# A two-layer hybrid trunk with a mixture of experts: layer 1 with 4 large and 12 small experts, down weights issued one position later, each tile's rows gathered, added and normed by itself

## The chip, the cores and the metric
The kernel runs on one core of one Trainium2 chip. The time is the device time of one execution in microseconds (us); the median of three runs is given. One more execution was recorded by the profiler, and all rows come from that one.

## The reference
Two layers are applied to 256 context tokens and 256 latent tokens of width 1024, all in float32. A layer has a mixing half (retention, Mamba-2 and neighbourhood attention behind one input projection, then an output projection) and a mixture of experts. The change is in the second half of each layer, and in the norm ahead of either half:

```
def moe_ffn(h, router_w, router_b, w_gate, w_up, w_down):
    ...
    for e in range(N_EXPERTS):
        he = jax.nn.silu(t @ w_gate[e]) * (t @ w_up[e])
        out = out + gates[:, e:e + 1] * (he @ w_down[e])
```

There are 16 experts with a hidden width of 512, and each token has two of them, so `gates` has two values that aren't zero in a row. `h` becomes `h + g_f * moe_ffn(modulate(rmsnorm(h)))`. Layer 0 does this for all 512 tokens, layer 1 for the 256 latent ones alone.

## The kernel before, in words
Tokens lie in tiles of 128 (`NT` = 4 tiles; `tiles(l)` gives 4 tiles in layer 0 and tiles 2 and 3 in layer 1). Semaphores order everything by hand; each engine has its own program.

*Routing.* `route` and `assign` (DVE) choose two experts for each token, count the tokens of each, and rank the experts by load; experts 0 and 1 are put at ranks 0 and 1 always, since their weights are loaded before the router has run. The first `BIG` = 8 ranks are large, with room for 128 tokens, the other 8 small, with room for 64 (`SMALL_CAP`). `rounds` (L1800) says how many rounds are needed until all tokens have had a place; `order_i` (L1806) lists the expert of each position, in one copy.

*Positions.* A round goes through 16 positions q. `RANKS` mixes them: two large, two small, and so on. Two small experts that stand side by side share one gather of 128 token rows; such a group, or one large expert, is a unit (`UNITS`, `NU` = 12). For each unit DVE finds the token of each slot (`slots_of`, `who`), POOL gathers the rows (`gather`, L2053), PE turns them (`turn_x`, L1037) and ACT copies them (L1343).

*PE in a round.* For each q, in this order: gate weights of q (`wide(r, q, 0)`), turning of the product of q-1 (`turn_h`, L1069), up weights of q (`wide(r, q, 1)`), at a unit's first position the turning of the next unit's rows, and down weights of q-1 (`down`). A large expert has 16 matmuls of 512 columns in each of gate (L1060), up (L1060) and down (L1087); a small one has its two halves side by side, gate and up at L1057 with 32 matmuls of 256 columns, down at L1082 with 16 of 512. ACT does silu and the copy of the turned product, DVE the product of gate and up (L1858) and the copy of the result (L1866); ACT then stores the rows of the result (L1365 in two pieces for a small expert, L1368).

*SP and the weights.* There are six slots of 2 MB: gate, up and down for even positions and the same for odd ones. The weights of position q+2 go where those of q were. The four loads that experts 0 and 1 can have early, and the last two of expert 0, are issued ahead of the round. Then a loop over pairs of positions reads the expert's number from `order_i` and, for gate, up and down in turn, waits until PE has finished that product of q-2 (`gate_pe`, `up_pe`, `dn_pe`) and issues the load (`load_expert`, L590). SP's instructions run in order, so a load also waits for the waits of all loads ahead of it.

*The end of a round.* When all rows are stored, POOL gathers for each tile its second choice, then for each tile its first (`sum_order`; two gathers per tile, four buffers, L2074). DVE adds each, times the token's gate, to `tokA`, which ACT has set to zero before the round (L1335, L1911). After the last round DVE multiplies each tile by the gate row (L1940), and the addition to `h` is done by POOL for even tiles (L2079) and DVE for odd ones (L1944).

*Norms.* `square_rows` (ACT, L1158) sums the squares of each tile; `norm_rows` (DVE) waits for all tiles, scales them (L1450), waits for POOL's power (`rsqrt`, L1978), and scales the tiles (L1454); PE then turns them (L683).

## Time and profile before

| | us |
|---|---|
| median of 3 runs | 1457.79 |
| the three runs | 1447.16, 1457.79, 1470.85 |
| the profiled execution | 1446.61 |
| its span, first to last instruction | 1444.8 |
| PE busy in the span | 1239.8 (86%) |
| weight loads of PE (beside its matmuls) | 673.2 |
| DVE, ACT, POOL busy | 409.9, 223.1, 139.9 |
| mean granted clock of PE | 0.931 of full |
| read from and written to HBM | 309.84 MB, 16.79 MB |

The experts of layer 0 run from about 469 to 777, their end with the next norm to 818, the experts of layer 1 from about 1112 to 1421 and their end to 1444.8. A busy PE is a PE with matmuls in flight. The granted clock is 1.00 at 2.4 GHz and 0.5 at 1.2 GHz; a stretch between them has both.

### The profile page before, as it was taken

The page shows a single profiled execution, that of the slowest core. Times are in us where ns is not written, and L with a number is a line of the kernel's source. Part 1 is how long each engine was busy: PE and PEld are TensorE (multiplying, and loading weights), DVE is VectorE, ACT ScalarE, POOL GpSimd, SP SyncE. Part 2 cuts the span into 40 slices and gives each one's busy share as a digit, 9 for nine tenths or more (in the row PEclk, how much of TensorE's full clock was granted, in tenths as well). Part 3 has the DMA queues.
Part 4 walks back from the last instruction along what each step waited for, and adds up shares of the span by engine and source line. Part 5 has one row for each costly group of instructions (what it writes and reads, how often), then busy time and mean ns, then how long its engine had stood idle before and what let it go on. Part 6 is the DMA issues. An engine that isn't in the chain of part 4 may idle for free.

```text
span 1444.8 us, 14245 instructions
## 1 busy us (share of the span) xinstructions
PE 1239.8 (86%) x5712; PEld 673.2 (47%) x5712; DVE 409.9 (28%) x737; ACT 223.1 (15%) x412; POOL 139.9 (10%) x119
## 2 busy tenths in 40 slices
PE   4999999999994798989894399989993999989892
PEld 1444446676543354545442256547642444535351
DVE  0130125863225312121102621247325110111103
ACT  2121121112204110101000212221213100101010
POOL 0002112620000100000002202114000000000001
PEclk8899998799997899999997699999996999999997
DMA  9311125434604469899988222245374389999984
GB/s 365 134 58 59 59 109 218 169 117 175 291 5 171 160 261 391 363 385 367 400 339 298 71 65 110 103 191 202 117 291 170 135 347 363 374 383 370 384 351 147
DMA packets 34238, 327.53 MB, mean 227 GB/s; under 512 B 5632, under 2 KB 5632, under 8 KB 16512
## 3 DMA queue, kind: packets, MB, share of 16 engines
q1 hardware_dynamic: 23328, 292.03, 50.8%
q0 software_dynamic: 5184, 18.88, 3.9%
q10 hardware_dynamic: 5664, 15.73, 2.8%
q8 instruction: 46, 0.75, 0.2%
q14 instruction: 16, 0.13, 0.0%
HBM read 309.84 MB, written 16.79 MB: 226 GB/s over the span
## 4 chain that ended last, share of the span: by engine, by line
PE 76%; DMA 11%; DVE 6%; ACT 3%; issue 2%; POOL 1%; SPq 1%; ACTq 0%; DVEq 0%; POOLq 0%
PE ps L1060 16%; PE ps L720 13%; PE ps L1087 7%; DMA ring<-in_w_gate 6%; PE ps L964 6%; PE ps L707 6%; PE ps L1057 4%; PE ps L653 3%; PE ps L1082 2%; PE ps L877 2%; DMA ring<-in_w_mod 2%; PE ps L1037 2%; PE ps L893 1%; PE ps L921 1%; PE ps L638 1%
## 5 line engine op out<-in xcount | busy, mean ns | idle before, releaser
L720 PE MATMUL ps<-ring,featT 128*128 128x512 f32 (+1 forms) x480 | 186.9, 550 | 0.0
L1060 PE MATMUL ps<-ring,arena 128*128 128x512 f32 x256 | 127.6, 658 | 27.9 <-DMA ring<-in_w_gate 25.5
L720 PEld LDWEIGHTS ps<-ring,featT 128*128 128x128 f32 x480 | 90.7, 190 | 92.3 <-issue 89.9
L1060 PE MATMUL ps<-arena 128*128 128x512 f32 x256 | 113.3, 595 | 2.4 <-ACT arena L1343 2.4
L1087 PE MATMUL ps<-arena 128*128 128x512 f32 x256 | 113.7, 597 | 0.0
L1858 DVE TENSOR_TENSOR arena<-arena,ps 128x512 f32<-128x512 f32 (+1 forms) x32 | 17.7, 555 | 338.1 <-PE ps L1060 237.2
L1060 PEld LDWEIGHTS ps<-ring,arena 128*128 128x128 f32 x256 | 53.1, 213 | 97.5 <-issue 66.7
L707 PE MATMUL ps<-featT,ring 128*128 128x512 f32 (+1 forms) x192 | 82.6, 589 | 2.3 <-ACT featT L1168 2.3
L964 PE MATMUL ps<-ring,featT 128*128 128x512 f32 x192 | 82.7, 592 | 0.0
L1866 DVE COPY arena<-ps 128x1024 f32<-128x1024 f32 (+1 forms) x32 | 30.6, 958 | 164.5 <-PE ps L1087 109.0
L2053 POOL DMA_INDIRECT arena<-ffn_rows,slot_i x24 | 23.7, 989 | 538.8 <-DVE slot_i L1850 538.8
L1060 PEld LDWEIGHTS ps<-arena 128*128 128x128 f32 x256 | 47.4, 190 | 60.9 <-issue 60.9
L1350 ACT ACTIVATE arena<-ps 128x512 f32<-128x512 f32 (+1 forms) x32 | 15.7, 490 | 377.5 <-PE ps L1060 214.9
L1087 PEld LDWEIGHTS ps<-arena 128*128 128x128 f32 x256 | 47.4, 190 | 54.3 <-issue 54.3
L1057 PE MATMUL ps<-arena 128*64 128x256 f32 x512 | 58.8, 382 | 7.5 <-DMA arena<-in_w_up 7.3
L683 PE MATMUL ps<-const,tokA 128*128 128x128 f32 x112 | 20.1, 358 | 49.2 <-DVE tokA L1454 47.5
L1082 PE MATMUL ps<-arena 128*64 128x512 f32 x256 | 58.3, 595 | 4.3 <-ACT arena L1357 4.3
L1057 PE MATMUL ps<-ring,arena 128*64 128x256 f32 x512 | 58.8, 382 | 0.0
L707 PEld LDWEIGHTS ps<-featT,ring 128*128 128x128 f32 x192 | 36.8, 194 | 46.0 <-issue 42.7
L964 PEld LDWEIGHTS ps<-ring,featT 128*128 128x128 f32 x192 | 36.5, 190 | 45.9 <-issue 45.9
L1057 PEld LDWEIGHTS ps<-arena 128*64 128x64 f32 x512 | 38.9, 137 | 28.0 <-issue 15.2
L653 PE MATMUL ps<-ring,silT 128*32 128x256 f32 (+1 forms) x656 | 50.7, 431 | 0.0
(276 smaller groups left out, 1403.0 us busy)
## 6 DMA issues: line engine op xcount, KB each, us to landing
arena<-in_w_down SPq DMA_DIRECT2D x32, 2048.0 KB, 11.1
ring<-in_w_mod SPq DMA_DIRECT2D x21, 2048.0 KB, 7.7
arena<-in_w_gate SPq DMA_DIRECT2D x16, 2048.0 KB, 13.9
arena<-in_w_up SPq DMA_DIRECT2D x16, 2048.0 KB
ring<-in_w_gate SPq DMA_DIRECT2D x16, 2048.0 KB, 14.3
ring<-in_w_up SPq DMA_DIRECT2D x16, 2048.0 KB, 18.8
ring<-in_w_in SPq DMA_DIRECT2D x10, 2048.0 KB, 8.0
ring<-in_w_out SPq DMA_DIRECT2D x4, 2048.0 KB, 8.1
```

Source lines behind the costliest of these rows:

```text
L653: i = mm(mod_row(l, u)[g:g + 32, :], silT[:, k, :], piece(q)[:, k, c:c + mod_width(l)], start=k < 4, stop=k >= 4)
L707: o = mm(bank[:, lo:TOK], W[:, k, c:c + P], featT[:, k, lo:TOK], start=k == 0, stop=k == KD - 1)
L720: o = mm(bank[:, lo:hi], featT[:, k, P * i:P * i + P], W[:, k, lo:hi], start=k == 0, stop=k == KD - 1)
L877: i = mm(ps[:, 6 + t // 2, 256 * (t % 2):256 * (t % 2) + 256], featT[:, k, P * t:P * t + P], nvw[:, k, :], start=k == 0, stop=k == KD - 1)
L964: i = mm(ps[:, 4 + n % 2, :], featT[:, k, P * t:P * t + P], piece(p)[:, k, :], start=k == 0, stop=k == KD - 1)
L1037: o = tr(ps[:, 5 + k // 4, P * (k % 4):P * (k % 4) + P], gathered[u % 2][:, P * k:P * k + P], ident)
L1057: o = mm(ps[64 * half:64 * half + 64, m, 0:256], X_[:, k, at:at + SMALL_CAP], W[:, k, 256 * half:256 * half + 256], start=k == 0, stop=k = ...
L1060: o = mm(ps[:, m, :], X_[:, k, :], W[:, k, :], start=k == 0, stop=k == KD - 1)
L1082: o = mm(ps[64 * out_half:64 * out_half + 64, 3, :], hT[:, b, 64 * half:64 * half + 64], W[:, k, 512 * out_half:512 * out_half + 512], sta ...
L1087: o = mm(ps[:, 3 + out_half, :], hT[:, k, :], W[:, k, 512 * out_half:512 * out_half + 512], start=k == 0, stop=k == 3)
L1866: V.tensor_copy(Yb[:, q % 2, 0:n], flat(3, n)).then_inc(S("y_dve"), 1)
L2053: G.indirect_dma_start(gathered[u % 2], None, rows_in[l], bass.IndirectOffsetOnAxis(slot_i[:, u % 2:u % 2 + 1], 0)).then_inc(S(f"gathered{ ...
```

## The change
There are three parts. (1) A `Plan` for each layer takes the place of `BIG`, `RANKS` and `UNITS`: layer 0 keeps its order, layer 1 has 4 large and 12 small experts, in 10 units. `Round` holds what the semaphores have counted before a round, as the layers now count differently. (2) SP issues the down weights of a position behind the gate and up weights of the next. (3) The rows come back tile by tile: ACT scales the row of the second choice into `tokA` (no zeroing any more), DVE adds the first choice, multiplies by the gate row and adds to `h`, within the round, for all tiles; POOL adds nothing. The norms split the tiles into all but the last and the last.

```diff
-BIG = 8
+BIGS = (8, 4)
...
-        UNITS = [u for j in range(NE // 4) for u in ((4 * j,), (4 * j + 1,), (4 * j + 2, 4 * j + 3))]
-        RANKS = [v for j in range(NE // 4) for v in (2 * j, 2 * j + 1, BIG + 2 * j, BIG + 2 * j + 1)]
-        NU = len(UNITS)
...
+            def units(self):
+
+                out, q = [], 0
+                while q < NE:
+                    n = 2 if self.small(q) else 1
+                    out.append(tuple(range(q, q + n)))
+                    q += n
+                return out
...
+            def runs(self):
+
+                starts = [q for q in range(NE) if q == 0 or self.ranks[q] != self.ranks[q - 1] + 1]
+                return [(a, b, self.ranks[a]) for a, b in zip(starts, starts[1:] + [NE])]
+
+        PLANS = (Plan(BIGS[0], [v for j in range(4) for v in (2 * j, 2 * j + 1, 8 + 2 * j, 9 + 2 * j)]),
+                 Plan(BIGS[1], [0, 1, 4, 5, 6, 7, 2, 3, 8, 9, 10, 11, 12, 13, 14, 15]))
...
-                with sp.Fori(1, R * (NE // 2)) as i:
-                    for c in range(2):
-                        e = sp.value_load(order_i[0:1, bass.ds((i % (NE // 2)) * 2 + c, 1)], min_val=0, max_val=NE - 1)
-                        for j, name in enumerate(("gate_pe", "up_pe", "dn_pe")):
-                            sp.wait_ge(S(name), first * NE + i * 2 + (c - 1))
-                            load_expert(e, c, j)
...
+                def wide_weights(behind, e, c):
+
+                    for j, name in enumerate(("gate_pe", "up_pe")):
+                        sp.wait_ge(S(name), first * NE + behind)
+                        load_expert(e, c, j)
+
+                def down_weights(behind, e, c):
+
+                    sp.wait_ge(S("dn_pe"), first * NE + behind)
+                    load_expert(e, c, 2)
+
+                wide_weights(1, expert_at(2), 0)
+                with sp.Fori(0, more * (NE // 2) + (NE // 2 - 2)) as i:
+                    e = [expert_at(i * 2 + 2 + n) for n in range(3)]
+                    wide_weights(i * 2 + 2, e[1], 1)
+                    down_weights(i * 2 + 1, e[0], 0)
+                    wide_weights(i * 2 + 3, e[2], 0)
+                    down_weights(i * 2 + 2, e[1], 1)
...
-                A(tokA[:, t0:NT, :].rearrange("p t (k c) -> p (t k) c", c=P), repeat(ONE, T * KD), ACT.Identity, scale=0.0
-                  ).then_inc(S("acc_zero"), 1)
...
+                    for i in range(T):
+                        t = t0 + i
+                        act.wait_ge(S(f"back{2 * i % 4}"), backs(l, 2 * i, first, n_round))
+                        A(tokA[:, t, :], back[2 * i % 4], ACT.Identity, scale=gate2[:, 1, t:t + 1]).then_inc(S("half_act"), 1)
...
-                V.tensor_copy(rounds[:, l:l + 1], few[:, 1:2]).then_inc(S("rounds_dve"), 1)
+                link(V.tensor_copy(rounds[:, l:l + 1], few[:, 1:2]))
+                V.tensor_scalar(rounds[:, DEPTH + l:DEPTH + l + 1], few[:, 1:2], -1.0, None, ALU.add).then_inc(S("rounds_dve"), 1)
...
-                V.tensor_copy(order_i.rearrange("p (j h c) -> p h j c", h=2, c=2),
-                              load_of.rearrange("p (h j c) -> p h j c", h=2, c=2)).then_inc(S("order_dve"), 1)
+                for a, b, v in plan.runs():
+                    i = V.tensor_copy(order_i[:, a:b], load_of[:, v:v + b - a])
+                i.then_inc(S("order_dve"), 1)
...
+                    for i in range(T):
+                        t, q = t0 + i, 2 * i + 1
                         dve.wait_ge(S(f"back{q % 4}"), backs(l, q, first, n_round))
+                        dve.wait_ge(S("half_act"), ended(l, first, n_round, i + 1))
+                        V.scalar_tensor_tensor(tokA[:, t, :], back[q % 4], gate2[:, 0, t:t + 1], tokA[:, t, :], ALU.mult, ALU.add
+                                               ).then_inc(S("both_dve"), 1)
+                        dve.wait_ge(S("both_dve"), ended(l, first, n_round, i + 1))
+                        V.tensor_tensor(tokA[:, t, :], tokA[:, t, :], grow[:, t // 2, :], ALU.mult).then_inc(S("gated_dve"), 1)
+                        dve.wait_ge(S("gated_dve"), ended(l, first, n_round, i + 1))
+                        V.tensor_tensor(h[:, t, :], h[:, t, :], tokA[:, t, :], ALU.add).then_inc(S("h_end"), 1)
...
-                    for q, (n, t) in enumerate(sum_order(l)):
-                        if q >= 4:
-                            pool.wait_ge(S("acc_dve"), added(l, first, n_round, q - 3))
+                    for q in range(2 * T):
+                        i, n = q // 2, 1 - q % 2
+                        if i >= 2:
+                            used = "half_act" if n else "both_dve"
+                            pool.wait_ge(S(used), ended(l, first, n_round, i - 1))
                             step_on()
...
-                for n in range(0, T, 2):
-                    pool.wait_ge(S("ffn_dve"), upto("ffn_dve", l, n + 1))
-                    G.tensor_tensor(h[:, t0 + n, :], h[:, t0 + n, :], tokA[:, t0 + n, :], ALU.add
-                                    ).then_inc(S("h_end0"), 1)
```

## Rows read from the trace of the kernel before
**Rows 1.** Waits of PE (engine, line, releaser: us, times, longest), 1120 to 1421, layer 1
```profile
PE ps L1060 <- DMA ring<-in_w_gate: 12.2, 3, 4.3
PE ps L1057 <- DMA arena<-in_w_up: 3.8, 3, 1.4
```
**Rows 2.** Waits of PE, 478 to 778, layer 0's experts
```profile
PE ps L1060 <- DMA ring<-in_w_gate: 13.4, 3, 5.4
PE ps L1057 <- DMA arena<-in_w_up: 3.5, 3, 1.4
```
**Rows 3.** PE in order of time (start, us, what), layer 1, positions 4 to 8
```profile
1194.14 9.93 PE L1060 MATMUL ps<-ring,arena 128*128 128x512 f32 x16 [3.92 <-DMA ring<-in_w_gate]
...
1215.67 7.13 PE L1060 MATMUL ps<-arena 128*128 128x512 f32 x16
...
1238.01 3.67 PE L1057 MATMUL ps<-ring,arena 128*64 128x256 f32 x32
...
1253.92 3.67 PE L1057 MATMUL ps<-arena 128*64 128x256 f32 x32
...
1259.12 3.67 PE L1057 MATMUL ps<-arena 128*64 128x256 f32 x32 [1.16 <-DMA arena<-in_w_up]
1262.60 3.63 PE L1082 MATMUL ps<-arena 128*64 128x512 f32 x16
1270.18 8.83 PE L1060 MATMUL ps<-ring,arena 128*128 128x512 f32 x16 [3.95 <-DMA ring<-in_w_gate]
...
1416.63 3.65 PE L1082 MATMUL ps<-arena 128*64 128x512 f32 x16 [2.12 <-ACT arena L1357]
```
**Rows 4.** SP's DMA issues in order of time, layer 1, positions 2 to 4
```profile
1161.85 0.33 SPq L590 DMA_DIRECT2D arena<-in_w_down  x1
...
1177.76 0.33 SPq L590 DMA_DIRECT2D arena<-in_w_down  x1
1179.46 0.34 SPq L590 DMA_DIRECT2D ring<-in_w_gate  x1
```
**Rows 5.** Windows of layer 1: us, busy by engine, then PEclk, DMA share, GB/s
```profile
1180.00:1213.00 33.00, 27.66 (x113) 13.63 (x111) 3.13 (x7) 2.54 (x5) 0.00 (x0) 0.90 0.99 415
1190.00:1202.00 12.00, 8.08 (x14) 3.48 (x13) 1.87 (x4) 0.00 (x0) 0.00 (x0) 0.72 1.00 426
1202.00:1212.00 10.00, 10.00 (x33) 4.92 (x31) 0.69 (x1) 0.87 (x2) 0.00 (x0) 1.00 1.01 434
```
**Rows 6.** DMA issues of layer 1's experts: count, KB each, us to landing
```profile
arena<-in_w_down SPq DMA_DIRECT2D x14, 2048.0 KB, 11.1
...
expert_rows<-arena ACTq DMA_DIRECT2D x8, 512.0 KB, 11.0
expert_rows<-arena ACTq DMA_DIRECT2D x14, 128.0 KB, 9.3
```
**Rows 7.** All engines in order of time, end of layer 0's experts
```profile
788.70 2.54 DVE L1911 SCALAR_TENSOR_TENSOR tokA<-arena,tokA 128x1024 f32<-128x1024 f32 x2 [0.81 <-DMA arena<-expert_rows,arena]
...
798.47 2.53 DVE L1911 SCALAR_TENSOR_TENSOR tokA<-arena,tokA 128x1024 f32<-128x1024 f32 x2 [0.75 <-DMA arena<-expert_rows,arena]
...
801.47 2.36 DVE L1940 TENSOR_TENSOR tokA<-tokA,arena 128x1024 f32<-128x1024 f32 x2 [0.22 <-DVE arena L1936]
...
809.42 3.25 DVE L1944 TENSOR_TENSOR h<-h,tokA 128x1024 f32<-128x1024 f32 x1
...
815.21 2.74 DVE L1454 TENSOR_SCALAR tokA<-h,stat 128x1024 f32<-128x1024 f32 x4 [1.16 <-POOL stat L1978]
...
818.00 5.12 PE L683 MATMUL ps<-const,tokA 128*128 128x128 f32 x32 [40.77 <-DVE tokA L1454]
```
**Rows 8.** All engines in order of time, end of layer 1's experts
```profile
1432.88 2.48 DVE L1911 SCALAR_TENSOR_TENSOR tokA<-arena,tokA 128x1024 f32<-128x1024 f32 x2 [0.57 <-DMA arena<-expert_rows,arena]
...
1438.19 3.25 DVE L1944 TENSOR_TENSOR h<-h,tokA 128x1024 f32<-128x1024 f32 x1
```
**Rows 9.** DVE, the router's chain of layer 0
```profile
463.21 0.17 DVE L1806 CAST order_i<-arena 128x16 int32<-128x16 f32 x1
```

More of the change, by code:

```diff
@@ L496, in opens, with ended, summed @@
-        def opens(q):
-            return q in [qs[0] for qs in UNITS]
-        def small(q):
-            return RANKS[q] >= BIG
-        def first_row(q):
-            v = RANKS[q]
-            return P * min(v, BIG) + SMALL_CAP * max(v - BIG, 0)
-        def stores(q):
-            return 16 * sum(2 if small(p) else 1 for p in range(q % 2, q + 1, 2))
-        STORES = stores(NE - 1)
+        def ended(l, first, n_round, n):
+            return first * NT + n_round * len(tiles(l)) + n
+        def summed(l, first, R, left=0):
+            return first * NT + R * len(tiles(l)) + (NT - left)
@@ L567, in _ @@
                     if l > 0 and m == 2:
-                        for w in ("h_end0", "h_end1"):
-                            sp.wait_ge(S(w), upto(w, l - 1, len(tiles(l - 1)) // 2))
+                        sp.wait_ge(S("h_end"), summed(l - 1, first, R))
                         layer_rows(l)
@@ L2089, in _ @@
                 if l > 0:
-                    for w in ("h_end0", "h_end1"):
-                        pool.wait_ge(S(w), upto(w, l - 1, len(tiles(l - 1)) // 2))
+                    pool.wait_ge(S("h_end"), summed(l - 1, first, R))
+                    pool.sem_inc(S("pool_steps"), 1)
                 for c in (0, CTX + 1):
```

269 lines of the change are left out of this document (150 added, 119 removed).

## The prediction
> **What bounds the kernel now.** I read four views in this order: who waited for whom on PE in the two expert stages, PE and SP in order of time over four expert positions, the windows with their DMA rate, and the two ends where the experts' rows are collected. The expert stages are the part that the change touches most, and they hold two fifths of the span. In layer 1 (1122 to 1421) PE waits 12.2 us for gate weights and 3.8 us for up weights, and in layer 0 13.4 and 3.5 us [rows 1, 2]. Nearly all else in the stage is PE work. The reader is to see the price of one period of four positions in [rows 3]: position 4 starts at 1194.14, position 8 at 1270.18. The stages of PE (gate of q, turning, up of q, down of q-1) cost, from start to start: a large expert behind a large one 22.3 us (1215.67 to 1238.01); a small one that opens a unit, behind a large one, 15.9 (1238.01 to 1253.92); a small one behind a small one 12.3 less a wait of 1.2, so 11.1; a large one behind a small one 21.5, less 2.8 that its gate took too long, so 18.7. Sum 68.0 us of PE work in a period of 76.0 (75.3 in the others). The gate that follows the wait of 3.9 us runs at 1.2 GHz for a while: 9.93 and 8.83 us where 7.1 is usual [rows 3], with the granted clock at 0.72 in that stretch and 1.00 in the next [rows 5]. So PE bounds the stage, with about 7 us of DMA wait and its clock loss in each period.
>
> Why do weights come late when transfers idle elsewhere? SP issues gate, up and down of position q+2 in that order, and each waits for its slot. At 1161.85, as PE ends down 0 and begins gate 2, SP issues the down weights of position 2; at 1177.76 those of position 3; and only 1.7 us later the gate of position 4 [rows 4]. PE had left that gate's slot when gate 2 was done, 3.67 us (a small gate [rows 3]) after 1161.85, at 1165.5. The gate load stood 14 us behind a down load that waited for PE's down 1.
>
> **Down weights one position later, both layers.** The new SP order (gate q+1, up q+1, down q) is the order in which PE leaves the slots, so nothing stands behind a wait that is not its own. It issues the same 42 loads; only the order and the addresses' register loads change, three of these at a loop's head, while SP waits for PE anyway (uncovered they would cost 1 us or so each time: the gap from down to the next gate is 1.7 us with one of them [rows 4]). No new wait stands on PE, ACT or DVE.
>
> Layer 0: what can go is 16.9 us of waits [rows 2] and three times 1.7 us of slow gate (8.83-7.13, from the gates in [rows 3]), 22.0 us. What is late next is the transfer rate. A period moves 12 loads of 2.097 MB, three gathers and two stores of 0.524 MB, and two stores of 0.262 MB (two pieces of 128 KB) [rows 6]: 28.3 MB. Busy stretches move 415 GB/s mixed and 434 with weights alone [rows 5], so 28.3/0.415 = 68.2 us against 68.0 of PE. That is a tie, but gate and up of positions 3 and 4 now leave some 10 to 15 us ahead, and a deficit of 0.2 us a period doesn't use this up. I take 21 us. Bounds: at 400 GB/s (4% under the 415, my low end for a queue that is never idle) a period needs 70.8 us and the gain is 22-8 = 14; it can't exceed 22.
>
> **Four large experts in layer 1.** Experts 0 and 1 always hold two of the four large places, so one round is enough only while the third largest of the other fourteen has at most 64 tokens. By the reference, the third largest load of all sixteen in layer 1 is 60, 44 and 43 for seeds 0, 1 and 2, so one round stays. Work removed on PE: positions 2 to 15 are now s s s s L L and eight s. With the stages above (an opening s behind s is 12.2: 11.1 and the turning of x): 15.9+11.1+12.2+11.1+18.7+22.3+15.9+11.1+12.2+11.1+12.2+11.1+11.1+11.1 = 187 us, where it was 231. From the end of down 0 at 1161.8 PE alone would end at 1349, and with the last turning and down (6 us) at 1355, against 1416.63+3.65 = 1420.3 now [rows 3, 4].
>
> But a small position releases its slots each 11 to 12 us and refills them with 6.29 MB, half a gather and a small store, 6.8 MB, 16.4 us at 415 GB/s. So transfers take over as the bound. In the times of before: the down load of position 2 is issued at 1161.85 as now; gate 4 and up 4 follow at 1165 and 1170; down 3 at 1177.76 starts at about 1178.7, and from there the queue always has a next load (in the two large stages PE takes 41.0 us where transfers need 2x17.7; the lead of 15 us from positions 3 to 5 covers the 5.6). Left then are 35 loads, 73.4 MB; five gathers, 2.6; stores of three large (1.6) and ten small positions (2.6): 80.2 MB. At 415 GB/s 193.3 us, so the last weights are in at 1372.0, PE sees them about 1 us later and needs 3.65 us for the last down: 1376.7. Gain 43.6; I take 43. Bounds: at 400 GB/s 200.5 us, gain 36; at 434 184.8 us, gain 52.
>
> A rule on this. Rows show 415 to 434 GB/s for HBM to SBUF with the engines' share at 0.99 to 1.01 [rows 5]. The Trainium skill (DMA: Bandwidth & Descriptors, Where 436 GB/s comes from) says that between HBM and SBUF the HBM side binds at some 358 GB/s and only the fabric reaches 435. By that rule 80.2 MB take 224 us and layer 1 gains 13 us instead of 43; the trace disagrees on this core with its 415, so it only makes one of the rivals.
>
> **Router's chain.** The order is copied in eight pieces in layer 0 and four in layer 1, in place of one of 0.17 us [rows 9], and the rounds get one more small instruction. At 0.1 us each, between nothing (they don't wait for one another) and 0.17: with the small one 0.9 and 0.5, on the path, since the first one-hot waits behind them; bounds 0.3 and 2.2 together. I take 1.5. The dropped zeroing on ACT ran beside this chain: nothing.
>
> **Rows gathered, added and normed by tile, end of layer 0.** Before, DVE takes the eight rows as they land, at 1.28 us each, and the last ends at 801.0; only then come the multiplications by the gate row (1.18 each) and the additions, at 3.25 each while POOL adds beside, up to 809.42+3.25 = 812.67; PE starts at 818.00 [rows 7]. After: ACT scales the first row of a tile, DVE does 1.28+1.18+an addition. Nothing shows an addition of this shape with POOL quiet: it lies between 1.18 (the multiplication, same shape) and 3.25; I take 1.2, as POOL no longer adds. Tile 0 can start at 788.70, when its second row is in; four tiles of 3.75 with their hand-overs end at 803.7. The last gathers wait for buffers as before and are in at about 800, hidden. Then square, power and one scaling (0.69 of the 2.74 for four [rows 7]) in place of four: 5.3 us become about 4.7, since three scalings still queue ahead on DVE. PE starts at 808.5 to 809. Gain 9, bounds 1 (additions of 3.25) and 11.
> The same split before each expert stage saves three and one scalings, less the queue: 1.1 and 0.7 us; bounds 0 and 3 together.
>
> **End of layer 1.** The last row is consumed at 1435.4, h is ready at 1441.4 [rows 8]. After: tile 0 (second row in at about 1431) ends at 1434.8, tile 1 at 1438.5. Gain 2.9, bounds -0.5 and 4.
>
> **Sum.** 43+21+9+1.8+2.9-1.5 = 76 us. The profiled execution took 1446.6, so 1370.4 for one like it. The three timed runs had a median of 1457.8, 11 us above it, and the lowest 1447.2 is at it. I put the new median at 1377, some half of that excess kept.
>
> **Rivals.** (A) As summed, 1377. (B) Transfers do worse when they are never idle (400 GB/s; a refill bubble of a microsecond in each position would do the same): 36+14+12 = 62 us, 1391. For it: a stretch with PE, gathers and stores at once moves 415, not 434. Against: the rate didn't fall within those stretches. (C) They do better, 434 as with weights alone: 52+22+13 = 87 us, 1366. Against: stores and gathers are always there. (D) HBM can't sustain the rate of a short stretch, and a period's mean of now, 28.3 MB in 75.3 us or 376 GB/s, is the ceiling: layer 1 needs 213 us for its 80.2 MB and gains 23, layer 0 nothing, the ends 12: 1457.8-35 = 1423. Against: 33 us on end at 415 [rows 5]. The page above gives such a ceiling; with its 358 the estimate would be 1433, within the bound of no change. (E) The clock, and this one ends on the other side. In layer 1 PE waits for every load, about 1.5 us three times a position. If this kept it at 1.2 GHz, small stages would take 22 us, above the 16.4 of the transfers: the twelve small stages, 187-41 = 146 us, become 292, and the stage ends near 1161.8+292+41+12 = 1507, 86 us later than before. With the other gains (33) that is 53 us over the median of before: 1511. Against no change it decides where the stage ends at 1420.3+33 = 1453, with 1453-1161.8-41-12 = 238 us for the 146: a granted clock near 0.6 over the small positions. For it: waits of 3.9 us brought 0.72 [rows 3, 5]. Against: the wait of 1.2 before an up and of 2.1 before the last down left 3.67 and 3.65 us, full speed [rows 3], and a PE that runs slower waits less. The Trainium skill (TensorE: Matmul & The Clock Gate, HAM oscillation — how this bites in real kernels) describes just such a loop, less work per load than wait, where each tile starts cold; by it E is what happens, by the short waits in the trace it isn't. (F) The change needs a second round in layer 1 after all: another 250 us, over 1620; it decides at 65 tokens for that third expert.
>
> **Chances.** A 0.57, B 0.20, C 0.15, D 0.04, E 0.03, F 0.01. A, B and C are faster by over 2% (29 us, about what a measurement of this kernel can tell from no change): 0.92 with them. So is most of D, to 1423; its lower ceilings are within 2%, and with the near side of E that makes 0.04. Slower, from E and F: 0.04. Range 1357 to 1402: from C with a run as fast as the profiled one, to B with all of the median's excess.
>
> **What would show it.** Right: in layer 0 no wait of PE for gate weights, and periods of 68 to 69 us; in layer 1 waits of 1 to 2 us before most products from about position 9 on, a DMA share of 0.98 or more with 410 to 420 GB/s from 15 us behind down 0 to the last load, a granted clock above 0.95, and a stage that is 43 us shorter; each tile's addition near 1.2 us, and PE in the next projection's turning some 9 us sooner behind the last down of layer 0. Wrong: waits for gathers or stores in place of those for weights, a rate of 400 GB/s or less, small gates of 7 us, additions of 3.25, or SP late at its loop's head.

## The result, and the profile after

The changed kernel takes 1375.07 us (median of 4 runs, 1366.9 to 1378.24), the kernel before 1454.97 in the runs beside it: a ratio of 0.9459, with a 95% interval of 0.9392 to 0.9526. Every ratio below is to the kernel before in the runs beside it. The forecast was 1377.0. The profiled execution took 1374.44 us, its span is 1372.6, 72.2 less than before, and its mean granted clock is 0.931 as before.

The span splits at events that both kernels have. "G1" is the gate product of a layer's second expert, which opens the steady part of the experts; "owner" is the first small matmul that finds a slot's token. The router's chain stands ahead of it, so its price is forecast in the rows that end at an owner.

| stretch of the span, us | before | after | gain | forecast |
|---|---|---|---|---|
| start to layer 0's first owner | 468.8 | 468.5 | 0.3 | 0.2 |
| owner to G1, layer 0 | 28.1 | 28.2 | -0.1 | 0 |
| G1 to the last down product, layer 0 | 280.4 | 258.1 | 22.3 | 21 |
| from there to PE's turning for the next norm | 40.8 | 31.0 | 9.8 | 9 |
| middle: from there to layer 1's first owner | 294.6 | 299.7 | -5.1 | 0.2 |
| owner to G1, layer 1 | 26.8 | 28.3 | -1.5 | 0 |
| G1 to the last down product, layer 1 | 280.8 | 237.1 | 43.7 | 43 |
| end of layer 1 | 24.5 | 21.6 | 2.9 | 2.9 |

The four large terms came within 1.3 us each; what was not forecast is the row of the middle stage, whose instructions are the same but for the split norm and the router's copies in its last part. Small rows are to be read with care: in ten profiles with the same code up to layer 0's first owner (the changed kernel and the experiments below that leave this stretch alone) it took 464.2 to 471.5 us, and one kernel had 470.8 and 464.2.

**Layer 0.** Waits of PE, 455 to 756 us (line, releaser: us in all, times, longest), which answer to [rows 2]:

```profile
PE ps L1091 <- DVE arena L1918: 13.9, 2, 11.3
PE ps L1076 <- DVE arena L1839: 5.9, 1, 5.9
PE ps L1100 <- DMA arena<-ffn_rows,slot_i: 2.6, 1, 2.6
PE ps L1123 <- ACT arena L1407: 2.4, 2, 1.2
PE ps L1145 <- ACT arena L1421: 2.1, 1, 2.1
```

No wait for a weight load is left: the 13.4 and 3.5 us of [rows 2] are gone. The first two lines are the router's chain, ahead of the experts. PE in order of time, at the start of two periods:

```profile
545.94 3.27 PE L1123 MATMUL ps<-ring,arena 128*128 128x512 f32 x7
...
613.92 2.41 PE L1123 MATMUL ps<-ring,arena 128*128 128x512 f32 x5
```

That is 68.0 us for four positions, where 76.0 stood in [rows 3] for layer 1 of before, and the window over it shows what carries it:

```profile
546.00:614.10 68.10, 68.10 (x301) 33.67 (x300) 13.53 (x20) 6.75 (x11) 2.81 (x3) 1.00 1.00 415
```

PE is busy for all 68.10 us at a granted clock of 1.00 while the DMA engines are at a share of 1.00 with 415 GB/s. It is the tie that the forecast described, with both sides busy throughout; these rows don't show which would end first.

**Layer 1.** Waits of PE, 1085 to 1347 us, which answer to [rows 1]:

```profile
PE ps L1145 <- DMA arena<-in_w_down: 6.6, 4, 2.6
PE ps L1120 <- DMA arena<-in_w_up: 3.8, 3, 2.2
PE ps L1100 <- DMA arena<-ffn_rows,slot_i: 3.3, 1, 3.3
PE ps L1120 <- DMA arena<-in_w_gate: 2.5, 2, 1.3
PE ps L1123 <- ACT arena L1407: 2.4, 2, 1.2
PE ps L1120 <- DMA ring<-in_w_gate: 2.3, 2, 1.2
PE ps L1120 <- DMA ring<-in_w_up: 2.3, 2, 1.1
```

PE in order of time, from position 11 on, and the end:

```profile
1267.61 3.67 PE L1120 MATMUL ps<-arena 128*64 128x256 f32 x32 [1.27 <-DMA arena<-in_w_gate]
...
1273.84 5.36 PE L1120 MATMUL ps<-arena 128*64 128x256 f32 x32 [2.18 <-DMA arena<-in_w_up]
...
1284.09 3.67 PE L1120 MATMUL ps<-ring,arena 128*64 128x256 f32 x32 [1.16 <-DMA ring<-in_w_gate]
...
1326.24 5.26 PE L1145 MATMUL ps<-arena 128*64 128x512 f32 x16 [2.64 <-DMA arena<-in_w_down]
...
1341.19 3.65 PE L1145 MATMUL ps<-arena 128*64 128x512 f32 x16 [1.68 <-DMA arena<-in_w_down]
...
1347.34 3.65 PE L1145 MATMUL ps<-arena 128*64 128x512 f32 x16 [2.12 <-ACT arena L1421]
```

The lead lasts until position 11, two later than forecast. From there PE waits 1.1 to 1.7 us before most products and still runs them at full speed (3.67 us), as [rows 3] had it; only behind the two longest waits, 2.18 and 2.64 us, does a product take longer (5.36 and 5.26 us). The first of these starts at full speed: the granted clock is 0.96 in its first 1.16 us and 0.52 in the 3.45 us after that. The windows of this stage:

```profile
1153.00:1345.00 192.00, 174.45 (x1060) 93.49 (x1056) 22.55 (x47) 16.52 (x32) 4.68 (x5) 0.98 1.00 424
1160.00:1340.00 180.00, 163.64 (x982) 87.75 (x978) 21.91 (x45) 15.78 (x30) 4.68 (x5) 0.98 1.01 427
```

The transfers hold 427 GB/s for 180 us, above the 415 of the sum.

**End of layer 0.** DVE, then PE, in order of time, which answer to [rows 7]:

```profile
766.24 1.28 DVE L1985 SCALAR_TENSOR_TENSOR tokA<-arena,tokA 128x1024 f32<-128x1024 f32 x1 [10.65 <-DMA arena<-expert_rows,arena]
767.56 1.22 DVE L1988 TENSOR_TENSOR tokA<-tokA,arena 128x1024 f32<-128x1024 f32 x1
768.82 1.22 DVE L1990 TENSOR_TENSOR h<-h,tokA 128x1024 f32<-128x1024 f32 x1
...
780.32 1.22 DVE L1990 TENSOR_TENSOR h<-h,tokA 128x1024 f32<-128x1024 f32 x1
...
783.08 2.74 DVE L1524 TENSOR_SCALAR tokA<-h,stat 128x1024 f32<-128x1024 f32 x4 [0.16 <-POOL stat L2048]
...
785.88 2.39 PE L744 MATMUL ps<-const,tokA 128*128 128x128 f32 x10 [31.03 <-DVE tokA L1524]
```

A tile takes 3.7 us on DVE, and the addition to `h` 1.22 us where it took 3.25 with POOL adding beside it. The Trainium skill (SBUF — State Buffer, SBUF: two separate sides) says that a DVE operation with two SBUF inputs and a GpSimd operation that reads SBUF take one port pair in turn, each for its whole length; the two durations agree with that, though no run here measured the port by itself. All four scalings still stand in one block behind the last tile, so splitting the norm saves only the square and power of three tiles.

**End of layer 1**, DVE, which answers to [rows 8]:

```profile
1362.03 1.28 DVE L1985 SCALAR_TENSOR_TENSOR tokA<-arena,tokA 128x1024 f32<-128x1024 f32 x1 [10.30 <-DMA arena<-expert_rows,arena]
...
1368.32 1.22 DVE L1990 TENSOR_TENSOR h<-h,tokA 128x1024 f32<-128x1024 f32 x1
```

### The profile page after: what moved, and what is told of

The parts are those of the page before. It is cut to its first block, busy times and chain, and to the rows that moved or that the text cites. A ratio compares the mean times of both kernels' runs of the same rounds, so it can differ in the third digit from the quotient of the medians.

```text
span 1372.6 us, 14516 instructions
## 1 busy us (share of the span) xinstructions
PE 1196.2 (87%) x5812; PEld 656.6 (48%) x5812; DVE 396.4 (29%) x742; ACT 221.3 (16%) x414; POOL 132.2 (10%) x118
## 4 chain that ended last, share of the span: by engine, by line
PE 79%; DMA 10%; DVE 6%; ACT 2%; issue 2%; POOL 1%; SPq 0%; ACTq 0%; DVEq 0%; POOLq 0%
PE ps L781 14%; PE ps L1123 13%; PE ps L1120 8%; PE ps L1150 6%; PE ps L1025 6%; PE ps L768 6%; PE ps L1145 4%; DMA arena<-in_w_down 4%; PE ps L714 3%; PE ps L938 2%; DMA ring<-in_w_mod 2%; DMA arena<-in_w_up 2%; PE ps L954 2%; PE ps L1100 2%; PE ps L982 1%
## 5 line engine op out<-in xcount | busy, mean ns | idle before, releaser
L1933 DVE TENSOR_TENSOR arena<-arena,ps 128x256 f32<-128x256 f32 (+1 forms) x32 | 16.7, 522 | 284.6 <-PE ps L1123 151.1
L1123 PE MATMUL ps<-ring,arena 128*128 128x512 f32 x192 | 90.1, 627 | 2.4 <-ACT arena L1407 2.4
L1123 PE MATMUL ps<-arena 128*128 128x512 f32 x192 | 84.9, 595 | 2.4 <-ACT arena L1407 2.4
L1150 PE MATMUL ps<-arena 128*128 128x512 f32 x192 | 85.3, 597 | 0.0
L1145 PE MATMUL ps<-arena 128*64 128x512 f32 x320 | 74.3, 607 | 10.9 <-DMA arena<-in_w_down 6.6
L1120 PE MATMUL ps<-arena 128*64 128x256 f32 x640 | 75.1, 388 | 6.3 <-DMA arena<-in_w_up 3.8
L1941 DVE COPY arena<-ps 128x512 f32<-128x512 f32 (+1 forms) x32 | 28.5, 892 | 159.3 <-PE ps L1150 81.3
L1414 ACT ACTIVATE arena<-ps 128x256 f32<-128x256 f32 (+1 forms) x32 | 14.8, 463 | 334.3 <-PE ps L1120 208.2
L1123 PEld LDWEIGHTS ps<-ring,arena 128*128 128x128 f32 x192 | 37.7, 201 | 51.0 <-issue 50.2
L1120 PEld LDWEIGHTS ps<-ring,arena 128*64 128x64 f32 x640 | 45.2, 137 | 33.2 <-issue 9.7
L1123 PEld LDWEIGHTS ps<-arena 128*128 128x128 f32 x192 | 35.5, 190 | 45.9 <-issue 45.9
L1150 PEld LDWEIGHTS ps<-arena 128*128 128x128 f32 x192 | 35.6, 190 | 40.6 <-issue 40.6
L744 PE MATMUL ps<-const,tokA 128*128 128x128 f32 x112 | 20.7, 367 | 37.9 <-DVE tokA L1524 36.2
```

Of the source, the lines that this page charges most:

```text
L1120: o = mm(ps[64 * half:64 * half + 64, m, 0:256], X_[:, k, at:at + SMALL_CAP], W[:, k, 256 * half:256 * half + 256], start=k == 0, stop=k = ...
L1123: o = mm(ps[:, m, :], X_[:, k, :], W[:, k, :], start=k == 0, stop=k == KD - 1)
L1145: o = mm(ps[64 * out_half:64 * out_half + 64, 3, :], hT[:, b, 64 * half:64 * half + 64], W[:, k, 512 * out_half:512 * out_half + 512], sta ...
L1150: o = mm(ps[:, 3 + out_half, :], hT[:, k, :], W[:, k, 512 * out_half:512 * out_half + 512], start=k == 0, stop=k == 3)
L1941: V.tensor_copy(Yb[:, q % 2, 0:n], flat(3, n)).then_inc(S("y_dve"), 1)
```

## The experiments

Each is the changed kernel with one edit, unless it says otherwise. Stretches are those of the table.

### One part undone at a time

**u_big8**: eight large experts in layer 1 again.

```diff
-BIGS = (8, 4)
+BIGS = (8, 8)
...
-                 Plan(BIGS[1], [0, 1, 4, 5, 6, 7, 2, 3, 8, 9, 10, 11, 12, 13, 14, 15]))
+                 Plan(BIGS[1], [v for j in range(4) for v in (2 * j, 2 * j + 1, 8 + 2 * j, 9 + 2 * j)]))
```

> The changed kernel with 8 large and 8 small experts in layer 1 too; the order of the loads and the ends stay changed. The stage of layer 1 is read from the start of position 1's gate to the end of position 15's down: 280.8 us before, 237.1 after. Theory (layer 0 bound by PE, layer 1 by transfers): layer 1 now runs as layer 0 does, 258 to 260 us, so the kernel is 22 us slower than the changed one, near 1396. Rival (layer 1 is bound by PE after the change too, and the plan's whole 44 us of PE work was its gain): stage 281, 1418.

Measured: 1397.61 us median, ratio 0.9639 (0.9598 to 0.9679). Layer 1's experts take 258.1 us instead of 237.1. A window of them:

```profile
1160.00:1340.00 180.00, 180.00 (x756) 87.63 (x753) 24.66 (x49) 17.68 (x29) 6.55 (x7) 1.00 1.00 419
```

PE is busy for 180 of 180 us and the DMA share is 1.00: with eight large experts layer 1 is the tie of layer 0. Beside the new order, four large experts are worth 21.0 us.

**u_oldorder**: gate, up and down of one position issued together again, with the rest of the change kept.

```diff
-                with sp.Fori(0, more * (NE // 2) + (NE // 2 - 2)) as i:
-                    e = [expert_at(i * 2 + 2 + n) for n in range(3)]
-                    wide_weights(i * 2 + 2, e[1], 1)
-                    down_weights(i * 2 + 1, e[0], 0)
-                    wide_weights(i * 2 + 3, e[2], 0)
-                    down_weights(i * 2 + 2, e[1], 1)
...
+                with sp.Fori(1, R * (NE // 2)) as i:
+                    for c in range(2):
+                        e = sp.value_load(order_i[0:1, bass.ds((i % (NE // 2)) * 2 + c, 1)], min_val=0, max_val=NE - 1)
+                        for j, name in enumerate(("gate_pe", "up_pe", "dn_pe")):
+                            sp.wait_ge(S(name), first * NE + i * 2 + (c - 1))
+                            load_expert(e, c, j)
```

> The changed kernel with the old order of loads in both layers (gate, up and down of a position together). Theory: layer 0 takes its load waits back, 280 us for the same stretch where the changed one has 258; layer 1, whose queue now has holes, takes 255 to 260 where the changed one has 237; in all 41 us slower, 1415. Rival (in layer 1 the transfers are the bound whatever the order, so the order pays in layer 0 alone): layer 1 237 to 240, 1397.

Measured: 1417.43 us median, ratio 0.9811 (0.9745 to 0.9878). Layer 0's experts take 284.3 us, layer 1's 257.1. PE's waits in layer 1, 1140 to 1425 us:

```profile
PE ps L1098 <- DMA ring<-in_w_gate: 12.0, 4, 4.1
PE ps L1098 <- DMA arena<-in_w_up: 8.9, 5, 2.4
PE ps L1098 <- DMA arena<-in_w_gate: 7.7, 4, 2.8
PE ps L1098 <- DMA ring<-in_w_up: 4.0, 3, 1.4
PE ps L1101 <- DMA ring<-in_w_gate: 3.1, 1, 3.1
```

The waits for gate weights are back, 22.8 us on three lines. Layer 1's 280.8 us of before fall to 258.1 by the order alone (u_big8), to 257.1 by the expert sizes alone (this kernel), and to 237.1 by both. So the two edits nearly add: 22.7 and 23.7 alone, 43.7 together. In layer 0 undoing the order costs 26.2 us, while making it won 22.3. This kernel's layer 0 is 3.9 us above that of before, at a granted clock of 0.964 against 0.982. The share not granted, times the stage, is 10.2 us against 5.0, so the clock can account for the 3.9; no run takes the two apart.

**u_oldend**: rows gathered second choice first and added as before, POOL adding even tiles, tokA zeroed, the norms in one group.

```diff
-                        A(tokA[:, t, :], back[2 * i % 4], ACT.Identity, scale=gate2[:, 1, t:t + 1]).then_inc(S("half_act"), 1)
...
+                for n in range(0, T, 2):
+                    pool.wait_ge(S("ffn_dve"), upto("ffn_dve", l, n + 1))
+                    G.tensor_tensor(h[:, t0 + n, :], h[:, t0 + n, :], tokA[:, t0 + n, :], ALU.add
+                                    ).then_inc(S("h_end0"), 1)
```

> The changed kernel with the rows added, gated and normed as before (zeroing on ACT, all second choices first, additions shared with POOL, one norm group). Theory: PE starts layer 1's turning 40.8 us behind layer 0's last down in place of 30.9, and the end of layer 1 takes 24.5 in place of 21.5; 13 us slower, 1387. Rival (what the ends save is eaten by the cold clock and by waits behind them): 5 us or less slower.

Measured: 1386.0 us median, ratio 0.9566 (0.9526 to 0.9606). The two ends take 40.7 and 24.6 us again, 9.7 and 3.0 more than after. But its middle stage takes 295.1 us, 4.6 less than after's 299.7, though the code there is the same except for the grouping of the norms. The middle stage was the open question from here.

### What bounds layer 1's experts now

**x_halfdown**: layer 1 loads half of each down weight from position 2 on.

```diff
-                    load_expert(e, c, 2)
+                    if l == 1:
+                        w = ins["w_down"][l, bass.ds(e, 1)].rearrange("o p c -> (o p) c")
+                        sp.dma_start(slots[3 * c + 2][:, 0:SLOT // 2], w[:, 0:SLOT // 2]).then_inc(S(f"slot{3 * c + 2}"), 16)
+                    else:
+                        load_expert(e, c, 2)
```

> The changed kernel, but in layer 1 the loads of the down weights from position 2 on bring only the first half of each row (1 MB in place of 2 MB), so the second half of the product uses old weights; PE does all its work. Theory (transfers bound the stage of layer 1, some 14.7 MB or 35 us less of them): the stage falls from 237 us until PE bounds it, 213 to 217 us, with no wait for weights, and the kernel takes 1351 to 1355. Rival (PE bounds it): 236 to 237, 1374.

Measured: 1352.85 us (one run), the stage 216.4 us instead of 237.1. A window of it:

```profile
1140.00:1300.00 160.00, 160.00 (x966) 83.97 (x964) 22.34 (x45) 16.15 (x30) 5.62 (x6) 1.00 0.98 402
```

With 14.7 MB fewer to read PE is busy throughout this window, and in the whole stage it waits 1.8 us for weights. So PE alone needs 216.4 us at most, and the other 20.7 are the transfers'. The forecast's sum for PE alone (end at 1355, from G1 at 1139.5) was 215.5.

**x_lesspe**: half the matmuls of layer 1's up products from position 2 on.

```diff
-                    for k in range(KD):
+                    nk = KD // 2 if l == 1 and m == 1 and q >= 2 else KD
+                    for k in range(nk):
```

> The changed kernel, but in layer 1 the up products from position 2 on take half of their matmuls (4 of 8 blocks of the input), so some 28 us of PE work are gone; all loads stay. Theory (transfers bound the stage): the stage stays within 3 us of 237 and the waits of PE for weights grow by what its work shrinks. Rival (PE bounds it): 210 to 215 us, 1350. A third, the clock: longer waits of PE bring it down to 1.2 GHz over most of the small positions; then matmuls at 1.2 GHz show in the last eight positions, and the stage is over 245.

Measured: 1373.72 us (one run), the stage 236.7 us. A window of it:

```profile
1160.00:1340.00 180.00, 145.15 (x784) 74.45 (x780) 21.08 (x44) 15.81 (x30) 4.68 (x5) 0.92 1.01 427
```

PE is busy 145.15 us, 18.5 fewer than after in the same window, at the same 427 GB/s, and nothing is won. The transfers bound the stage, shown from both sides. The granted clock was 0.92 in this window against 0.98: more waiting costs clock, and costs no time, since the clock is not what the stage waits for. The waits of this run also show that their length does not settle whether a slow product follows:

```profile
1262.42 5.35 PE L1146 MATMUL ps<-arena 128*64 128x512 f32 x16 [1.89 <-DMA arena<-in_w_down]
...
1340.29 3.65 PE L1146 MATMUL ps<-arena 128*64 128x512 f32 x16 [3.54 <-DMA arena<-in_w_down]
```

**x_straight**: layer 1's positions in order of rank, the four large ones first.

```diff
-                 Plan(BIGS[1], [0, 1, 4, 5, 6, 7, 2, 3, 8, 9, 10, 11, 12, 13, 14, 15]))
+                 Plan(BIGS[1], list(range(16))))
```

> The changed kernel with layer 1's positions in order of rank: L L L L, then twelve small, in place of L L s s s s L L and eight small. The work of PE and the bytes are the same. Theory (transfers bound it, and the queue is full only as far as PE releases slots): the large positions release slots late, the queue has holes in the first 80 us, and the stage takes 245 to 249 us, the kernel 10 us more. Rival 1 (PE bounds): no change, 237. Rival 2 (transfers bound it whatever the order, the bytes alone count): no change either, but with the queue as full as before.

Measured: 1386.3 us (one run), the stage 248.3 us. Its windows:

```profile
1112.00:1160.00 48.00, 46.81 (x138) 22.87 (x137) 7.23 (x14) 5.24 (x7) 2.81 (x3) 1.00 0.82 308
1160.00:1350.00 190.00, 162.97 (x1078) 92.41 (x1076) 21.81 (x46) 16.41 (x32) 4.70 (x5) 0.99 1.00 413
```

The changed kernel has this in the first of the two windows:

```profile
1112.00:1160.00 48.00, 46.81 (x232) 24.85 (x232) 7.09 (x15) 5.88 (x9) 2.81 (x3) 1.00 0.87 344
```

With the large experts first, slots come free more slowly: 308 instead of 344 GB/s over 48 us, 1.7 MB less, which is 4 us at 427 GB/s, and the next 190 us move 413 where the changed kernel has 425 in a like window. The stage is 11.2 us longer, and the two losses in bytes come to some 9 us of it (1.7 and 2.3 MB at 427 GB/s). Four small positions ahead of the last two large ones let the loads run ahead; the work on PE is the same.

### Where the middle stage's 5 us went

**v_warm**: matmuls whose output nobody uses, before and between the owner products and ahead of layer 1's mixing norm, to have PE's clock at 2.4 GHz when the work comes.

```diff
+            def warm(n):
+                for _ in range(n):
+                    mm(ps[:, 0, :], ident, const[:, 0:512], start=True, stop=True)
```

> The changed kernel with idle matmuls on PE (identity by constants, into a bank that nothing reads) where PE waits before work that now runs at 1.2 GHz: nine before each expert stage, 3, 4 and 2 between its first small steps, and nine before layer 1's first turning. Theory (the cold clock costs 2.4 us at the first gate and up of layer 0's experts, 3 in layer 1's, 2 to 2.5 in the turning behind layer 0): the first gate and up take 14.0 to 14.5 us in place of 16.4 and 17.0, and the kernel is 6 to 8 us faster than the changed one, near 1367. Rival (the clock isn't brought up by these, or they come in the way of what PE waits for): no change, or up to 5 us slower.

Measured: 1377.59 us median, ratio 0.9497 (0.9413 to 0.9582); the profiled execution took 1369.63. In that one the two stretches from owner to G1 take 25.4 and 25.1 us instead of 28.2 and 28.3, and the middle 297.5 instead of 299.7 at a clock of 0.960. The medians of the runs don't tell the kernel from the changed one, so this is no version that beats it. The trace shows what holds it back, as both the theory and its rival are true in part. The clock is up when the experts' work comes, but the nine idle matmuls ahead of layer 1's experts start late, and PE still has them when DVE has made the row for the first owner:

```profile
1073.95 10.02 PE L1087 MATMUL ps<-const 128*128 128x512 f32 x18 [4.77 <-issue]
1083.80 0.28 PE L1102 MATMUL ps<-const,arena 128*128 128x1 f32 x2
```

```profile
1078.03 0.42 DVE L1933 TENSOR_REDUCE arena<-arena 128x128 f32<-128x256 f32 x1
```

The row is ready at 1078.45 and the owner starts at 1083.80, 5.3 us later, where the changed kernel starts it at once; in layer 0 it is 4.2 us (468.04 and 472.27). So 2.8 and 3.2 us are won behind the owner and more is lost ahead of it. The profile is 4.8 us under the changed kernel's for two reasons: 2.2 us in the middle stage, whose clock doesn't fall at about 202 us here, and 3.2 behind layer 1's owner, while G1 of layer 0 is 0.9 later. One of the six runs took 1542.01 us, at a mean granted clock of 0.811 where the others have 0.944 to 0.956; no profile of it was kept, and its cause is open.

The trace's clock records show what differs. In both kernels the stage's instructions come one like the other until, in after only, the granted clock falls again about 202 us into the stage. The share of the clock that was not granted, times the stage's length, is 14.1 us in before (0.952) and 20.1 in after (0.933): 6.0 us more, against the 5.1 by which the stage is longer. The windows from 201 to 241 us after the stage's start (PE busy, weight loads, DVE, ACT, POOL, then PEclk, DMA share, GB/s), before and then after, the latter with the 56 us ahead of it:

```profile
1019.00:1059.00 40.00, 37.45 (x268) 24.15 (x268) 12.85 (x22) 10.09 (x27) 0.00 (x0) 1.00 0.56 215
```

```profile
930.88:986.88 56.00, 53.80 (x459) 39.80 (x454) 36.59 (x55) 9.04 (x20) 15.05 (x11) 1.00 0.54 207
986.88:1026.88 40.00, 37.96 (x261) 25.10 (x260) 12.23 (x21) 9.57 (x28) 0.00 (x0) 0.87 0.45 171
```

Ahead of it the two are alike (1.00 in the 56 us before, as in before); then 0.87 stands against 1.00. Two theories: P, that it is the place of the stage against the moments at which the granted clock can change; E, that the new row end itself leaves something behind. The next three kernels ran beside each other.

**x_delay1** and **x_delay2**: the scaling of the first tile done two or four times more ahead of layer 1's mixing norm (the diff is of x_delay1; x_delay2 has `range(4)`).

```diff
                     dve.wait_ge(S(which + "_rs"), upto(which + "_rs", l, m + 1))
+                    if which == "a" and l > 0 and m == 0:
+                        for _ in range(2):
+                            link(V.tensor_scalar(tokA[:, 0, :], h[:, 0, :], stat2[:, 0:1], None, ALU.mult))
```

> The changed kernel with the scaling of the first tile (0.75 us) done twice more ahead of layer 1's mixing norm: the middle stage (from PE's turning of layer 1's norm to the first owner matmul of layer 1's experts) starts about 1.6 us later than it would, with nothing else changed. In six profiles with the new row end that stage took 298.6 to 301.2 us at a granted clock of 0.931 to 0.934; in the two with the old end 294.6 and 295.1 at 0.952 and 0.951, with the same instructions. Theory P (place): what differs is where the stage lies against the moments at which the granted clock can change; 1.6 us later brings it near the place that the old end gives. Expected: the stage at about 295 us and a clock near 0.95, without the fall at about +202 us, and the whole near 1371 us although work was added. Theory E (the new end itself leaves something behind, as in its split norm or the gathers' order): the stage stays at 299 to 301 us at 0.933, the whole near 1376.

> As the last, with the scaling done four times more, some 3.1 us. Theory P: this brings the stage to about the same place against the clock's changes as the changed kernel has without a delay, so the stage is long again, 299 to 301 us at about 0.933, the whole near 1377 us. Theory E: the same 299 to 301 us. A theory that any delay helps (the DVE or a DMA being late, say) would have it near 295 us here too.

**a_again**: the changed kernel, unchanged.

> The changed kernel once more, unchanged, to see how much its stages vary from one profiled execution to the next. Theory P: the middle stage's length goes with its place in this execution, 299 to 301 us where that is as before, 295 where the stage happens to start 1 to 2 us later or earlier against the clock's changes; the other stages within 2 us of the first profile. Theory E: 299 to 301 us.

Measured (one run each): x_delay1 1372.63 us with a middle stage of 298.7 us at 0.934; x_delay2 1373.56 with 293.6 at 0.953; a_again 1375.36 with 298.6 at 0.934. Both delays came out the other way than expected of P. E as stated fails too, since the new end stands in front of 293.6 us. The delays had not landed where they were meant to: PE's turning began only 0.5 us later behind the last down product in x_delay1 (31.5 against 31.0), as the last rows happened to be in sooner, and 2.4 later in x_delay2. What goes with the stage's length in all of these is how long after its start the clock first falls: 136.0 to 136.2 us in the short ones, 137.5 to 138.8 in the long ones. That gave a sharper test.

**o_delay**: u_oldend with two more scalings, so the old end moved. **x_delay2b**: x_delay2 once more, with timed runs.

> The kernel with the old row end (u_oldend) and the scaling of the first tile done twice more (about 1.6 us) ahead of layer 1's mixing norm. So far the middle stage took 293.6 to 295.1 us in three profiles, the ones in which the granted clock first falls 136.0 to 136.2 us after the stage's start (kernel before, old end, and the new end with four more scalings), and 298.6 to 301.2 us in the eight in which it first falls 137.5 to 138.8 us after it (all with the new end, two of them the changed kernel itself). Theory P (place against the clock's changes): the old end, started 1.6 us later, gets a first fall near +137.5 to +138.5, then the further ones near +202 and +237, and its stage goes from 295 to 299 to 301 us at about 0.933, the whole near 1393. Theory E (the new end itself makes the stage long, and four scalings happened to mend it): the old end keeps 295 us at 0.95, the whole near 1388.

> The changed kernel with four more scalings (3.1 us, of which 2.5 reached PE the first time) once more. Theory P: the stage near 294 us again where the clock first falls near +136.2 in this execution (the starts of one kernel's stages vary by some 0.3 us against the clock's changes), 299 to 301 where it first falls at +137 or later. By its stages the kernel takes 1372 to 1376 us: 2.5 later at the norm, 5 to 6 less in the middle stage, so 1 to 4 us under the changed kernel's 1375, less than its runs spread. Theory E: a stage of 294 us here again, whatever the place.

Measured: o_delay 1405.94 us (one run), middle stage 313.2 us at 0.892. x_delay2b 1382.89 us median, ratio 0.9485 (0.9418 to 0.9551), its profiled execution 1386.54 with a middle stage of 313.0 us at 0.893, where the same kernel had 293.6. The windows from 201 to 241 us after the stage's start, of x_delay2 and then of x_delay2b:

```profile
992.68:1032.68 40.00, 37.45 (x269) 24.09 (x268) 12.97 (x22) 10.10 (x27) 0.00 (x0) 1.00 0.56 215
```

```profile
986.41:1026.41 40.00, 39.43 (x165) 24.49 (x166) 8.21 (x13) 6.18 (x18) 0.00 (x0) 0.53 0.17 59
```

and of u_oldend and then of o_delay:

```profile
1001.26:1041.26 40.00, 37.45 (x269) 24.12 (x268) 12.95 (x22) 10.10 (x27) 0.00 (x0) 1.00 0.56 216
```

```profile
1002.66:1042.66 40.00, 39.52 (x165) 24.55 (x166) 8.20 (x13) 6.09 (x18) 0.00 (x0) 0.53 0.18 59
```

One kernel has both outcomes, 165 matmuls against 269 in the same 40 us, and the old end, moved, has the long one. The granted clock accounts for it: the share not granted, times the stage, is 13.8 us in x_delay2 and 33.5 in x_delay2b, 19.7 more, and the stage is 19.4 longer. Thirteen profiled executions by their first fall (v_warm is left out, since it changes what PE does there):

| clock first falls, us into the stage | kernel | middle stage, us |
|---|---|---|
| 136.0 | before | 294.6 |
| 136.2 | u_oldend, x_delay2 | 295.1, 293.6 |
| 137.5 to 137.8 | after, a_again, x_delay1, u_oldorder | 299.7, 298.6, 298.7, 298.6 |
| 138.0 to 138.8 | x_straight, x_halfdown, u_big8, x_lesspe | 300.3, 300.8, 301.2, 299.6 |
| 138.6, 138.7 | o_delay, x_delay2b | 313.2, 313.0 |

E falls: the new end stands in front of 293.6 us and the old one in front of 313.2. P fits the direction of all thirteen, eleven of which it was drawn from, but both last runs were expected at 299 to 301 us and took 313, so its size was missed. The size does not follow from the first fall alone: near 138.6 stand 301.2 and 313.2. What sets apart a second fall of 6.8 us from one of 37.5 us stays open. The two stages of 313 us are also the only two profiled on their chip, and one chip against another was not tried; against it, the kernel before takes 1449.43 us there, as in the runs beside the other experiments (1449.84 and 1449.77), and x_delay2b itself has a run of 1373.05 there.

## Why the prediction was right, and where it was not

- **Layer 0's experts** (21, measured 22.3). Right in mechanism and size: no wait for weights, a period of 68.0 us as forecast, a tie of PE and transfers. The gain is 0.3 above what was called its upper bound, but the same code of layer 0 took 258.1 us in three profiles and 259.8 to 260.2 in nine, so the gain is 20.2 to 22.3, with the size of the difference in one fall of the clock at the last product.
- **Layer 1's experts** (43, measured 43.7). The mechanism, transfers as the bound, is shown by x_halfdown and x_lesspe, the rate by the window. That it came so close is in part luck, as errors in the sum cancelled. Set back by the 25.5 us that G1 came sooner, the forecast had the transfers busy from 1153.2 to 1346.5 with 80.2 MB at 415 GB/s. They moved 192x0.424 = 81.4 MB from 1153 to 1345, and the last product then did not wait for its weights but for ACT's copy of the turned product (2.12 us at 1347.34), a hand-over that was there before [rows 3] and that the sum had not added. The turned product is ready at about 1345.2, but ACT's program first issues the two stores of position 14's result (1345.70 to 1346.80) and copies at 1346.90; no run has the other order. Rivals B, C and D were rivals on this rate: 427 and 424 lie between A and C, and D, a ceiling of 376 or the 358 that the prediction priced with it, is out. The Trainium skill itself has the better rule in Perfetto Trace Analysis (Roofline): a core that is alone at its memory may go up to some 435 GB/s, the sum of its 16 DMA engines; the 427 agree with that.
- **Rival E** (the clock kept at 1.2 GHz). Its loop did not close: the stage's granted clock is 0.986. Waits of 1.1 to 1.7 us left full speed. Two waits of 2.2 and 2.6 us were followed by a slow product, once each, and the transfers went on meanwhile. x_lesspe, with 26.3 us of waits for down weights alone, came to 0.92 in its window, still far from 0.6.
- **End of layer 0** (9, measured 9.8) and **end of layer 1** (2.9, measured 2.9). The addition of 1.22 us was the term with the wide bounds (1.18 to 3.25), and it is at its low end.
- **Norm split and the router's chain** (+1.8 and -1.5). PE begins layer 0's expert norm at 437.29, 1.2 us sooner than before, as forecast (1.1). But the first owner is only 0.3 us sooner. The order's eight copies cost 0.66 us in all, 0.5 more than the one of [rows 9], the extra instruction on the rounds 0.2, and 0.35 is lost as DVE takes up the counts from PE (457.67 against 458.56, where PE's matmul was 1.24 sooner). So the chain cost 0.7 in layer 0, where the sum had 0.9. In the sum these terms were a gain of 0.3, and they measure -1.3 over the stretches around them, middle stage aside. Nearly all of that is layer 1's stretch from owner to G1, 28.3 us at a granted clock of 0.73 where before had 26.8 at 0.77: 7.6 us not granted against 6.2. The granted clock accounts for this too, and the changed kernel itself had 27.3 at 0.76 the second time (a_again).
- **The step that failed** is one that the prediction did not have: that a stage whose instructions stay the same takes the same time. The middle stage took 5.1 us longer. By the last five experiments this is no price of the new row end; the same kernel has 293.6 or 313.0 us there, and the clock not granted accounts for the difference. Where the stage lands against the clock's changes goes with its length, by up to 20 us. In their profiles the kernel before had one of the short places, after a middling one. How often each kernel lands where was not measured. Single stages of the timed runs were not recorded, but their mean granted clock was: the changed kernel's fastest run, 1366.9, has 0.940 and its slowest, 1378.24, has 0.928; for x_delay2b it is 1373.05 at 0.937 and 1393.89 at 0.922.
- **Rivals D and E** were priced from the median of 1457.8, A, B and C from 1453.2 (the profiled execution with 6.6 of the excess). On the base of the others D is 1418 and E 1506, which changes no verdict.

Profile against profile the sum was 76 us and 72.2 came: 78.7 in the four large terms instead of 75.9, and 6.4 lost in the rows that were to bring 0.3. The median of the runs, 1375.07, is 0.6 above the profiled execution, where the forecast had kept 6.6 of the excess of before: that was too much by 6.0, and by luck it made up for the missing 4.

## What to carry to other kernels

Issue loads in the order in which the consumer frees their slots; a queue that runs in order turns one early wait into a stall for everything behind it, and here undoing it cost 26.2 us in layer 0 and 20.0 in layer 1. When an edit makes the compute shorter, work out the bytes of the stage and a sustained rate next: that sum, not the removed work, gave layer 1's time (216.4 us for PE alone, but 237.1 for the stage), and both edits were needed, as each alone gave only half. Matmuls that only keep the clock up need an end that is sure to come before the work does; here they held up the first owner by 4.2 and 5.3 us. Before a few microseconds in an untouched stage are put down to an edit, profile the same kernel again, and move the stage by a microsecond or two.

## What the runs showed of the hardware that was not expected

- The same instructions took 293.6 and 313.0 us in one kernel, and the difference is granted clock (0.953 and 0.893). It goes with how long after the stage's start the clock first falls (136.2 and 138.7 us). The Trainium skill (TensorE: Matmul & The Clock Gate, Part 1: The HAM clock gate) says that the monitor behind the clock runs freely and doesn't reset with the kernel; these profiles agree with it as far as they go, and what they add is a stage in the middle of a long kernel; no run here shows the monitor itself.
- A PE that is busy does not get its clock back at once. In x_delay2b it is busy 39.43 of 40 us in the window above, and the granted clock over it is 0.53.
- Short waits are free where transfers bound the stage. Seven waits of 1.1 to 1.3 us between small products left them at 3.67 us. Longer ones have both outcomes: a product of 5.36 us follows 2.18 us and one of 5.35 follows 1.89 (x_lesspe), while 3.65 follows 2.12 and 3.54 (x_lesspe).
- One core kept 427 GB/s of weight loads, gathers and stores together for 180 us on end, with PE at work beside them, against 415 in a stretch of 33 us before the change [rows 5].
